# Later places in the instruction order for weight splits, and earlier places for two norm products, in a two-block transformer layer

## Chip, core and metric

The kernel runs on one core of a Trainium2 chip. The metric is the device time of one execution in microseconds (us), lower is better; before is the kernel as it stood, after the kernel with the change. The engines are PE (matmul), PEld (its weight load), DVE (vector), ACT (scalar), POOL (GpSimd) and SP, whose queue here issues the weight loads.

## What is computed

Two blocks one after the other on 512 tokens of width 1024, float32 in and out. Only what the change touches:

```python
# first block, after its mixers
x = x + gate1 * (concat([o_g, o_s]) @ w_out)              # w_out 1024 x 1024
h2 = rms_norm(x, norm2_w) * (1.0 + scale2) + shift2
ffn = (silu(h2 @ w_gate) * (h2 @ w_up)) @ w_down          # 1024 -> 2816 -> 1024
x = x + gate2 * ffn
# second block, with 16 meta tokens ahead of the 512
h = rms_norm_2(concat([meta, x]), pre_norm_g)
z = h @ w_in_2                                            # then split in column groups
(pv, pg, cq, ckv, kr, mg, cu, cg, sbcx, sg, gl) = split_cols(z)
a, gate = split(cu, 2); z = a * sigmoid(gate)             # conformer branch
```

## The kernel before, in words

**Precision by splitting.** Every big float32 product is made of three fp32r matmuls. A weight panel of 128 x 2048 lies in one of three ring buffers; ACT copies it, rounded, to `whi` (`split_hi`, L1422), and DVE subtracts to get `wlo` (`split_lo`, L1932). There are two pairs `whi`/`wlo`, used in turn. `split_hi` and `split_lo` take no name: each call takes the next panel of one fixed list (here `out2`, `out3`, `g0`, `u0`, `g1`, `u1`, `g2`, ...), and it stands in the engine's own order wherever the call stands. Before it writes, ACT waits until PE's last product with the panel two earlier is done (`used`). PE waits for `w_lo` of a panel in `project` (L564) and `first_tiles` (L656). SP loads the panel three later once `w_lo` of a panel is done. Activations are split in the same way (`hi_part` L1426 on ACT, `lo_part` L1937 on DVE).

**Stage A, output projection and second norm.** PE makes eight tiles `mo` 0 to 7 of 128 x 512: 0 to 3 with `out0` and `out1` (L959), 4 and 5 with `out2`, 6 and 7 with `out3` (L569). For each m DVE adds the residual (L2286), ACT squares it (L1660) and writes the rounded, unnormed row `raw_hi` (L1444), POOL adds the squares up (L1349), DVE writes the rest of the row (`raw_rest`, L2005) and goes to m + 1. `out2` is split ahead of m = 0 on ACT and after the residual of m = 0 on DVE.

**A projection ahead of its norm.** The first gate panel `g0` is multiplied with the unnormed rows, chunk by chunk, so that PE has work while the norm is found. Between its chunks PE makes the sums (`norm_stats`, L583 and L586, after chunk 1) and spreads the factor over the partitions (`norm_spread`, L593, after chunk 3). DVE then makes the normed rows (L1996), ACT scales and rounds them (L1433, L1426), DVE makes the rests (L1937), and PE multiplies them with `u0` (L662). The product of `g0` is multiplied by the factor afterwards, in `gate_first_out`, from a copy that ACT takes out of PSUM (`factor_out`, L1441), behind the split of `g1`.

**Stage B, third norm and first panels of the second block.** The same for `cug` (unnormed rows, four tiles `cgate` of 264 columns) and `cu` (normed rows, four tiles). `first_tiles` opens all its PSUM banks before its first matmul. The eight banks go round, and of the four that `cu` opens the last two are those of `cgate` (0,0) and (0,1). Before, ACT copies the four `cgate` tiles out behind its sixth normed row (`both`, L1707), and DVE multiplies the copies by the factor, straight from its PSUM bank, behind all its rests (L2358).

Of the kernel before, what the change touches and what calls it, by code (L numbers as in the profile page):

```python
# [16 lines left out]
D = 1024  # L17
# [98 lines left out]
def program(nc, a, out, known):  # L116
# [3 lines left out]
    with ctx:  # L120
# [13 lines left out]
        def done(stage, *index):  # L134

            return sem(stage), (known[(stage,) + index] if known else 1)
# [128 lines left out]
        hpre3 = arena[:, 0:KD * T].rearrange("p (k t) -> p k t", k=KD)  # L265
        raw3 = arena_r[:, 22 * T:22 * T + 2 * KD * TM].rearrange("p (s k t) -> p s k t", s=2, k=KD)

        factor_of = {"2": arena[:, 36 * T:37 * T]}

        def raw2(s, k):  # L270
            tile = 16 + k if s else k if k < 4 else 8 + k
# [1114 lines left out]
        def _(act):  # L1386
# [28 lines left out]
            def root(tag, out, key, scale, bias):  # L1415
                act.wait_ge(*filled(*key))
                A(out, bank(*key)[0:out.shape[0], 0:out.shape[1]], ACT.Sqrt, bias=bias, scale=scale).then_inc(*read(*key))
# [6 lines left out]
            def hi_part(stage, index, dst, src):  # L1424

                A(dst, src, ACT.Copy).then_inc(*signal(stage + "_hi", *index))  # L1426
# [232 lines left out]
                    act.wait_ge(*done("sqsum" + tag, m - 2))  # L1659
                A(hsq[m % 2] if m else sacc, xT[:, m, :], ACT.Square).then_inc(*signal("xsq" + tag, m))  # L1660

            split_hi()
            for m in range(KD):
                act.wait_ge(*copied("mo", m))
                square_of("2", m)
                act.wait_ge(*done("dve_vectors", "modA2"))
                raw_hi("2", m, modA2[:, m:m + 1])
                if m in (2, 5, 7):
                    split_hi()
            root("2", sroot, ("sum2",), 1.0 / D, epsc)  # L1670
            modulate("2", modA2, 24)
            split_hi()
            factor_out("2")
            for part, (c0, n) in enumerate(FFN_PARTS):
                for i in range(c0 // 2, (c0 + n) // 2):
                    for k in (2 * i, 2 * i + 1):
                        act.wait_ge(*filled("fg", k))
                        if k >= 2:
                            act.wait_ge(*done("a", k - 2))
                        if k < 2:  # L1680
                            act.wait_ge(*copied("fg", k))
                            act.wait_ge(*copied("gshift"))
                            A(silug[k], silug[k], ACT.Silu, bias=gate_bias0[:, k:k + 1]).then_inc(*signal("silug0", k))
                        else:
                            A(silug[k % 2], bank("fg", k)[:, :], ACT.Silu).then_inc(*read("fg", k))
                    if i:
                        split_hi()
                    for k in (2 * i, 2 * i + 1):
                        act.wait_ge(*copied("fu", k))
                        hi_part("a", (k,), act_split[:, 0, k - c0, :], silug[k % 2])  # L1690
                    split_hi()
                for m in range(KD):
                    act.wait_ge(*copied("fd", part, m))
                    if part:
                        if m == 0:
                            for dst in (h_split, raw3):
                                A(dst[:, 0, :, 0:META], hmeta.rearrange("p (k t) -> p k t", k=KD), ACT.Copy)\
                                    .then_inc(*signal("meta_hi"))
                        square_of("3", m)
                        raw_hi("3", m, V1[:, V1_ROWS["pre"] + m:V1_ROWS["pre"] + m + 1])  # L1700
                    split_hi()
            H2 = TM // 2

            def both(key, dst, func=ACT.Copy):
                for half in range(2):
                    act.wait_ge(*filled(*key, half))
                    A(dst[:, half * H2:(half + 1) * H2], bank(*key, half)[:, 0:H2], func).then_inc(*read(*key, half))  # L1707

            root("3", sroot, ("sum3",), 1.0 / D, epsc)
            for k in range(KD):  # L1710
                act.wait_ge(*done("xn3", k))
                hi_part("h3", (k,), h_split[:, 0, k, real], hpre3[:, k, :])
                if k == 5:
                    for m in range(2):
                        both(("cgate", m), conf_gate[m])


            for m in range(2):
                act.wait_ge(*done("cscaled", m))
# [191 lines left out]
        def _(dve):  # L1911
# [76 lines left out]
            def normed_and_rest(tag, first_out, weight=None):  # L1988

                dve.wait_ge(*filled("spread" + tag))  # L1990
                src = bank("spread" + tag)[:, :]
                for k in range(KD + AHEAD):
                    if k < KD:
                        ins = (stt(out=pre_of(tag, k), in0=xT[:, k, :], scalar=col(weight, k), in1=src,
                                   op0=ALU.mult, op1=ALU.mult) if weight else
                               tt(pre_of(tag, k), xT[:, k, :], src, ALU.mult))  # L1996
                        ins.then_inc(*signal("xn" + tag, k))
                    if k >= AHEAD:
                        h_rest(tag, [k - AHEAD])
                first_out()  # L2000

            def raw_rest(tag, k, weight):
                hi = raw_of(tag, 0, k)
# [284 lines left out]

            for m in range(KD):
                residual(("mo", m), m, 16)  # L2290
                if m == 0:
                    split_lo()
                raw_rest("2", m, modA2[:, m:m + 1])
                if m in (3, 5):
                    split_lo()
                if m == 5:
                    dve.wait_ge(*loaded("g0"))
                    for k in range(KD):
                        wk, shift = W("g0")[:, k, :], modT[:, 24 + k:25 + k]
                        if k:  # L2300
                            dve.wait_ge(*done("gate_acc", k - 1))
                            ins = stt(out=gate_acc, in0=wk, scalar=shift, in1=gate_acc, op0=ALU.mult, op1=ALU.add)
                        else:
                            ins = ts(gate_acc, wk, shift, None, ALU.mult)
                        ins.then_inc(*signal("gate_acc", k))

            def gate_first_out():

                split_lo()
                dve.wait_ge(*copied("spread2"))  # L2310
                dve.wait_ge(*filled("gshift"))
                v.tensor_copy(gate_bias0, bank("gshift")[:, 0:2]).then_inc(*read("gshift"))
                for k in range(2):
                    dve.wait_ge(*filled("fg", k))
                    last = tt(silug[k], bank("fg", k)[:, :], factor_of["2"], ALU.mult)
                    last.then_inc(*read("fg", k))

            spread("2", diag)
# [1 line left out]
            normed_and_rest("2", gate_first_out)  # L2320
            for part, (c0, n) in enumerate(FFN_PARTS):
                for i in range(c0 // 2, (c0 + n) // 2):
                    if i:
                        split_lo()
                    if i in (1, 3):
                        ada_sum(10 + i // 2)
                    for k in (2 * i, 2 * i + 1):
                        dve.wait_ge(*(done("silug0", k) if k < 2 else copied("fg", k)))
                        dve.wait_ge(*filled("fu", k))
                        tt(silug[k % 2], bank("fu", k)[:, :], silug[k % 2], ALU.mult).then_inc(*read("fu", k))  # L2330
                    for k in (2 * i, 2 * i + 1):
                        lo_part("a", (k,), act_split[:, 1, k - c0, :], silug[k % 2], act_split[:, 0, k - c0, :])
                    split_lo()
                    if i == 5:
                        ada_mod(10)
                        ada_mod(11)
                        dve.wait_ge(*copied("ada", 11))
                for m in range(KD):
                    residual(("fd", part, m), m, 40)
                    if part:  # L2340
                        if m == 0:
                            dve.wait_ge(*done("meta_hi"))
                            for dst in (h_split, raw3):
                                tt(dst[:, 1, :, 0:META], hm, dst[:, 0, :, 0:META].bitcast(F32), ALU.subtract)\
                                    .then_inc(*signal("h3meta"))
                        raw_rest("3", m, col("pre", m))
                    if not part or m < KD - 1:
                        split_lo()

            H2 = TM // 2  # L2350

            def conf_first_out():

                for m in range(2):
                    for half in range(2):
                        dve.wait_ge(*copied("cgate", m, half))
                    scaled = conf_gate[m][:, META:TM]
                    tt(scaled, scaled, bank("spread3")[:, :], ALU.mult).then_inc(*signal("cscaled", m))  # L2358
                for m in range(2):
                    dve.wait_ge(*done("cscaled", m))  # L2360
                v.engine_nop().then_inc(*read("spread3"))

            spread("3", diag3)
            split_lo()
# [275 lines left out]
```

## Time and profile before

| | us |
|---|---|
| median of 3 executions | 1339.77 |
| lowest, highest | 1338.87, 1343.93 |
| the profiled execution | 1338.87 |
| its span, first to last instruction | 1337.1 |
| PE busy, share of span | 95% |
| mean granted PE clock | 0.985 of full speed |

The page also shows DVE busy for 52% of the span, ACT 37%, PEld 75% and POOL 9%. A busy share is an average over stages. What a moved instruction costs is read from the stretch in which it stands: what PE waits for there, and when. Stage A lies at 362 to 424 us of the span, stage B at 762 to 790 us.

### The profile page before, as it was taken

How to read it: one execution, taken by the hardware profiler on the slowest of the kernel's cores; microseconds unless marked ns; L12 is line 12 of the kernel's file. 1: busy time of each engine (PE TensorE's matmuls, PEld its weight loads, DVE VectorE, ACT ScalarE, POOL GpSimd, SP SyncE). 2: the span in 40 equal slices, each digit the busy share in tenths (PEclk: the TensorE clock that was granted, in tenths of full speed). 3: DMA queues.
4: the chain of work that ended last, by engine and by line, in shares of the span. 5: the costliest groups of instructions: out<-in, count | busy, mean ns of one | idle time of the engine just before them, and what ended most of it. 6: DMA issues, size and time to landing. Idle time of an engine off the chain costs nothing.

```text
span 1337.1 us, 20515 instructions
## 1 busy us (share of the span) xinstructions
PE 1275.0 (95%) x8676; PEld 1008.2 (75%) x8676; DVE 697.3 (52%) x1038; ACT 490.1 (37%) x822; POOL 115.9 (9%) x133
## 2 busy tenths in 40 slices
PE   3899999999989999999999999999899989999996
PEld 2577878889878888888888897986466657677675
DVE  5699878654466443333334588575644333333324
ACT  3544543664345232222223442234445532222232
POOL 4000006411020000000000100000022210000001
PEclk9899999999999999999999999999899999999999
DMA  8665610002022542343322433231301053333211
GB/s 296 217 202 182 220 63 35 3 4 66 1 95 91 162 150 71 95 126 95 95 61 83 140 100 95 86 88 38 71 1 52 1 138 83 83 83 83 83 63 63
DMA packets 141210, 125.77 MB, mean 94 GB/s; under 512 B 6728, under 2 KB 124769, under 8 KB 140992
## 3 DMA queue, kind: packets, MB, share of 16 engines
q1 hardware_dynamic: 137856, 119.62, 29.4%
q0 software_dynamic: 1520, 2.49, 0.6%
q10 hardware_dynamic: 1744, 2.36, 0.5%
q8 instruction: 69, 1.13, 0.4%
q14 instruction: 21, 0.17, 0.0%
HBM read 121.77 MB, written 2.10 MB: 93 GB/s over the span
## 4 chain that ended last, share of the span: by engine, by line
PE 85%; DVE 7%; ACT 3%; DMA 2%; issue 2%; POOL 0%; ACTq 0%; SPq 0%; DVEq 0%; POOLq 0%
PE bank L569 52%; PE bank L810 7%; PE bank L1154 5%; PE bank L662 5%; PE bank L1225 3%; PE bank L1182 2%; PE bank L1136 2%; PE bank L1108 2%; DMA arena<-in_meta_tokens_dram 1%; PE bank L959 1%; DVE wlo L1932 1%; PE bank L1120 1%; PE bank L760 1%; PE bank L782 1%; PE bank L769 1%
## 5 line engine op out<-in xcount | busy, mean ns | idle before, releaser
L569 PE MATMUL bank<-hsplit,whi 128*128 128x512 f32 (+1 forms) x1872 | 561.4, 384 | 0.8 <-DVE wlo L1932 0.7
L569 PEld LDWEIGHTS bank<-hsplit,whi 128*128 128x128 f32 x1872 | 341.6, 188 | 82.3 <-issue 19.0
L569 PE MATMUL bank<-hsplit,wlo 128*128 128x512 f32 (+1 forms) x936 | 352.3, 376 | 0.0
L1932 DVE TENSOR_TENSOR wlo<-ring,whi 128x2048 fp32r<-128x2048 f32 (+4 forms) x90 | 186.6, 2073 | 169.6 <-ACT whi L1422 169.4
L569 PEld LDWEIGHTS bank<-hsplit,wlo 128*128 128x128 f32 x936 | 175.9, 188 | 32.9
L1422 ACT ACTIVATE whi<-ring 128x2048 fp32r<-128x2048 f32 (+4 forms) x90 | 156.3, 1737 | 103.1 <-DVE xT L2286 52.9
L569 PE MATMUL bank<-a_split,whi 128*128 128x512 f32 x340 | 104.7, 389 | 0.0
L2577 DVE TENSOR_TENSOR arena<-bank,tb 128x512 f32<-128x512 f32 x24 | 16.6, 692 | 126.1 <-PE bank L1154 106.2
L1154 PE MATMUL bank<-arena,ring 128*128 128x512 f32 x160 | 75.8, 606 | 1.3 <-DVE arena L2536 1.1
L569 PEld LDWEIGHTS bank<-a_split,whi 128*128 128x128 f32 x340 | 63.8, 188 | 13.2
L1849 ACT ACTIVATE tb<-bank,V 128x512 f32<-128x512 f32 x30 | 20.5, 683 | 138.9 <-PE bank L569 138.9
L569 PE MATMUL bank<-a_split,wlo 128*128 128x512 f32 x170 | 66.1, 389 | 0.0
L1961 DVE SCALAR_TENSOR_TENSOR post<-ring,small,post 128x512 f32<-128x512 f32 x77 | 57.9, 752 | 3.5 <-DMA ring<-in_w_ada_dram 0.8
L1349 POOL TENSOR_TENSOR acc<-acc,tb 128x512 f32<-128x512 f32 x12 | 15.6, 1298 | 434.6 <-ACT tb L1660 434.6
L1154 PEld LDWEIGHTS bank<-arena,ring 128*128 128x128 f32 x160 | 30.1, 193 | 28.6 <-issue 26.5
L1426 ACT ACTIVATE a_split<-tb 128x512 fp32r<-128x512 f32 x22 | 13.8, 632 | 88.4 <-DVE tb L2330 88.3
L2519 DVE TENSOR_TENSOR arena<-arena,consts 128x128 f32<-128x128 f32 x32 | 9.5, 298 | 70.2 <-ACT arena L1818 47.2
L1182 PE MATMUL bank<-hsplit,whi 128*128 128x512 f32 x128 | 44.9, 432 | 0.0
L2286 DVE SCALAR_TENSOR_TENSOR xT<-bank,small,xT 128x512 f32<-128x512 f32 x24 | 17.9, 748 | 50.1 <-PE bank L569 40.1
L1225 PE MATMUL bank<-whi,m_split 128*128 128x512 f32 x128 | 39.6, 390 | 1.7 <-DVE m_split L1937 1.7
L2398 DVE SCALAR_TENSOR_TENSOR arena<-arena,V 128x512 f32<-128x512 f32 x60 | 40.3, 745 | 0.0
L2330 DVE TENSOR_TENSOR tb<-bank,tb 128x512 f32<-128x512 f32 x22 | 14.9, 690 | 48.5 <-PE bank L569 47.0
(430 smaller groups left out, 1786.6 us busy)
## 6 DMA issues: line engine op xcount, KB each, us to landing
ring<-in_w_ada_dram SPq DMA_DIRECT2D x24, 1024.0 KB, 5.3
ring<-in_w_in_dram SPq DMA_DIRECT2D x22, 1024.0 KB, 5.3
ring<-in_w_in_dram SPq DMA_DIRECT2D x34, 512.0 KB, 5.5
ring<-in_w_gate_dram SPq DMA_DIRECT2D x11, 1024.0 KB, 5.3
ring<-in_w_up_dram SPq DMA_DIRECT2D x11, 1024.0 KB, 5.3
ring<-in_w_down_dram SPq DMA_DIRECT2D x8, 768.0 KB, 4.8
ring<-in_w_down_dram SPq DMA_DIRECT2D x8, 640.0 KB, 4.3
ring<-in_w_out_dram SPq DMA_DIRECT2D x4, 1024.0 KB, 5.2
```

Source lines behind the costliest of these rows:

```text
L569: last = mm(o[0:m, 0:n], w[:, k, c0:c0 + m], rhs(s, k), start=k + i == 0, stop=k == kn - 1 and i == 2)
L662: last = mm(o[:, 0:n], w[:, k, c0:c0 + P], rhs(s, k), start=at + i == 0, stop=at == len(order) - 1 and i == 2)
L810: last = mm(o[r, i * width:(i + 1) * width], left[r, n, :], right(n)[r], start=start, stop=stop)
L1108: mm(o[:, 0:m0], q_mla[0:QD, h, i * WIN:(i + 1) * WIN], k_mla[0:QD, h, 0:m0], start=True, stop=True)\
L1136: mm(o[p * HD:(p + 1) * HD, pair * WIN:(pair + 1) * WIN], v_mla[:, c, h * HD:(h + 1) * HD], mpT[u % 2][:, c * WIN:(c + 1) * WIN], start=c ...
L1154: last = mm(o[:, :], W(name)[:, k0 + k, :], ybr[:, kb + k, :], start=k == 0, stop=k == nk - 1)
L1182: last = mm(early[0][:, :], w[:, k, P * (b % 2):P * (b % 2) + P], hx(s, k), start=k + x == 0, stop=k == KD - 1 and x == 2)
L1225: last = mm(fo[b][:, :], mix_split[:, s, 4 * kp + k, b * P:(b + 1) * P], w[:, k, :], start=kp + k + i == 0, stop=kp == 1 and k == 3 and i ...
L1422: split_hi = splitter(act, lambda hi, src: A(hi, src, ACT.Copy), None)
L1932: split_lo = splitter(dve, None, lambda lo, src, hi: tt(lo, src, hi, ALU.subtract))
L1961: last = stt(out=acc, in0=w[:, k, :], scalar=c, in1=acc, op0=ALU.mult, op1=ALU.add)
L2398: stt(out=conf_sum[:, m, :], in0=src, scalar=tap, in1=conf_sum[:, m, :], op0=ALU.mult, op1=ALU.add))
```

## The change

The number of splits and the order of the panels stay. Their places move: `out2` is split after m = 1 on both engines (ACT `m in (1, 3, 5, 7)`, DVE `(1, 3, 5)`), `out3` on ACT after m = 3 rather than m = 2, and `g1` inside the first turn of the FFN loop, on ACT behind the two Silu of that turn and on DVE behind both products with the factor.

The products with the factor (`first_out`) move forward: in `normed_and_rest` they stand ahead of the last two rests, and wait there for ACT's copy of the factor. Stage B gets such a copy too (`factor_of["3"]`). `conf_first_out` now reads `cgate` directly from its four PSUM banks, in halves, multiplies by the copy and so releases the banks on DVE; 16 meta columns are copied unscaled. ACT's four copies of `cgate` are gone.

```diff
-        factor_of = {"2": arena[:, 36 * T:37 * T]}
+        factor_of = {"2": arena[:, 36 * T:37 * T], "3": arena[:, 8 * T:9 * T]}
...
-            split_hi()
             for m in range(KD):
                 act.wait_ge(*copied("mo", m))
                 square_of("2", m)
                 act.wait_ge(*done("dve_vectors", "modA2"))
                 raw_hi("2", m, modA2[:, m:m + 1])
-                if m in (2, 5, 7):
+                if m in (1, 3, 5, 7):
                     split_hi()
             root("2", sroot, ("sum2",), 1.0 / D, epsc)
             modulate("2", modA2, 24)
-            split_hi()
             factor_out("2")
...
-                    if i:
-                        split_hi()
+                    split_hi()
                     for k in (2 * i, 2 * i + 1):
                         act.wait_ge(*copied("fu", k))
...
+            root("3", sroot, ("sum3",), 1.0 / D, epsc)
+            for k in range(KD):
+                act.wait_ge(*done("xn3", k))
+                hi_part("h3", (k,), h_split[:, 0, k, real], hpre3[:, k, :])
+            factor_out("3")
...
-            root("3", sroot, ("sum3",), 1.0 / D, epsc)
-            for k in range(KD):
-                act.wait_ge(*done("xn3", k))
-                hi_part("h3", (k,), h_split[:, 0, k, real], hpre3[:, k, :])
-                if k == 5:
-                    for m in range(2):
-                        both(("cgate", m), conf_gate[m])
...
+                    if k == KD + 1:
+                        dve.wait_ge(*copied("spread" + tag))
+                        first_out(factor_of[tag])
                     if k >= AHEAD:
                         h_rest(tag, [k - AHEAD])
-                first_out()
...
                 residual(("mo", m), m, 16)
-                if m == 0:
-                    split_lo()
                 raw_rest("2", m, modA2[:, m:m + 1])
-                if m in (3, 5):
+                if m in (1, 3, 5):
                     split_lo()
...
-            def gate_first_out():
-
-                split_lo()
-                dve.wait_ge(*copied("spread2"))
+            def gate_first_out(factor):
+
                 dve.wait_ge(*filled("gshift"))
...
-                    if i:
-                        split_lo()
+                    split_lo()
                     if i in (1, 3):
...
-            def conf_first_out():
+            def conf_first_out(factor):
 
                 for m in range(2):
                     for half in range(2):
-                        dve.wait_ge(*copied("cgate", m, half))
-                    scaled = conf_gate[m][:, META:TM]
-                    tt(scaled, scaled, bank("spread3")[:, :], ALU.mult).then_inc(*signal("cscaled", m))
-                for m in range(2):
-                    dve.wait_ge(*done("cscaled", m))
-                v.engine_nop().then_inc(*read("spread3"))
+                        dve.wait_ge(*filled("cgate", m, half))
+                        o, at = bank("cgate", m, half), half * H2
+                        skip = 0 if half else META
+                        if skip:
+                            v.tensor_copy(conf_gate[m][:, 0:META], o[:, 0:META]).then_inc(*signal("part"))
+                        last = tt(conf_gate[m][:, at + skip:at + H2], o[:, skip:H2], factor[:, at + skip - META:at + H2 - META], ALU.mult)
+                        last.then_inc(*read("cgate", m, half))
+                    dve.wait_ge(*copied("cgate", m, 1))
+                    v.engine_nop().then_inc(*signal("cscaled", m))
```

## Rows read from the trace of the kernel before

**Rows 1.** The page's chain that ended last: share of the span by engine

```profile
PE 85%; DVE 7%; ACT 3%; DMA 2%; issue 2%; POOL 0%; ACTq 0%; SPq 0%; DVEq 0%; POOLq 0%
```

**Rows 2.** PE's waits, whole span: who for whom, us in total, times, longest

```profile
PE bank L769 <- POOL wscratch L1306: 3.3, 2, 3.1
...
PE bank L583 <- POOL acc L1349: 2.1, 1, 2.1
...
PE bank L586 <- ACT tb L1660: 1.4, 1, 1.4
```

**Rows 3.** Timeline of DVE, stage A: start, duration, line; idle time before, releaser

```profile
362.44 0.75 DVE L2286 SCALAR_TENSOR_TENSOR xT<-bank,small,xT 128x512 f32<-128x512 f32 x1 [3.30 <-PE bank L959]
365.07 2.29 DVE L1932 TENSOR_TENSOR wlo<-ring,whi 128x2048 fp32r<-128x2048 f32 x1 [1.88 <-ACT whi L1422]
...
367.94 0.75 DVE L2286 SCALAR_TENSOR_TENSOR xT<-bank,small,xT 128x512 f32<-128x512 f32 x1
370.01 1.27 DVE L2005 SCALAR_TENSOR_TENSOR a_split<-xT,small,a_split 128x512 fp32r<-128x512 f32 x1 [1.32 <-ACT a_split L1444]
371.20 0.74 DVE L2286 SCALAR_TENSOR_TENSOR xT<-bank,small,xT 128x512 f32<-128x512 f32 x1
```

**Rows 4.** Timeline of ACT, same stretch

```profile
368.72 0.63 ACT L1660 ACTIVATE tb<-xT 128x512 f32<-128x512 f32 x1 [2.55 <-DVE xT L2286]
369.26 0.71 ACT L1444 ACTIVATE a_split<-xT,small 128x512 fp32r<-128x512 f32 x1
```

**Rows 5.** Timeline of PE: first matmuls of tiles mo 4 and mo 6

```profile
368.36 0.62 PE L569 MATMUL bank<-hsplit,whi 128*128 128x512 f32 x2
...
380.15 0.70 PE L569 MATMUL bank<-hsplit,whi 128*128 128x512 f32 x2 [0.75 <-DVE wlo L1932]
```

**Rows 6.** Windows: PE, PEld, DVE, ACT, POOL busy (instructions); PE clock, DMA share, GB/s

```profile
227.90:234.70 6.80, 6.63 (x78) 4.91 (x78) 4.55 (x15) 2.37 (x8) 4.05 (x6) 0.50 0.01 4
...
398.60:405.40 6.80, 6.80 (x22) 5.74 (x22) 3.92 (x7) 1.95 (x2) 0.00 (x0) 0.50 0.04 5
```

**Rows 7.** Chain that ended last, 398 to 425 us: start, length, matmuls

```profile
400.51 5.19 PE bank L662 x12
...
406.59 2.75 PE bank L662 x12
...
409.68 13.72 PE bank L662 x60
```

**Rows 8.** Timeline of ACT, end of stage A

```profile
417.18 1.90 ACT L1422 ACTIVATE whi<-ring 128x2048 fp32r<-128x2048 f32 x1
418.99 0.57 ACT L1441 ACTIVATE arena<-bank 128x512 f32<-128x512 f32 x1
422.15 1.28 ACT L1683 ACT_TABLE_LOAD   x1 [2.59 <-DVE tb L2315]
423.44 1.34 ACT L1683 ACTIVATE tb<-tb,small 128x512 f32<-128x512 f32 x2
```

**Rows 9.** Timeline of DVE, end of stage A

```profile
406.63 2.48 DVE L1996 TENSOR_TENSOR arena<-xT,bank 128x512 f32<-128x512 f32 x4 [2.49 <-PE bank L593]
...
416.79 1.29 DVE L1937 TENSOR_TENSOR hsplit<-arena,hsplit 128x512 fp32r<-128x512 f32 x2 [0.53 <-ACT hsplit L1426]
...
421.40 1.28 DVE L2315 TENSOR_TENSOR tb<-bank,arena 128x512 f32<-128x512 f32 x2
```

**Rows 10.** Timeline of stage B: PE's first matmul of cu

```profile
777.89 0.48 PE L662 MATMUL bank<-hsplit,whi 128*128 128x264 f32 x2 [1.05 <-ACT arena L1707]
```

**Rows 11.** Timeline of stage B: ACT's last rounded row

```profile
778.83 0.63 ACT L1426 ACTIVATE hsplit<-arena 128x512 fp32r<-128x512 f32 x1 [0.24 <-DVE arena L1994]
```

**Rows 12.** Timeline of DVE, stage B: rests, and four PSUM products of 264 columns

```profile
778.72 2.48 DVE L1937 TENSOR_TENSOR hsplit<-arena,hsplit 128x512 fp32r<-128x512 f32 x4
...
788.79 1.57 DVE L2407 TENSOR_TENSOR arena<-bank,arena 128x264 f32<-128x264 f32 x4 [1.51 <-PE bank L662]
```

**Rows 13.** Chain that ended last, stage B: the matmuls of cu

```profile
777.89 11.88 PE bank L662 x96
```

More of the change, by code:

```diff
@@ L2314, in gate_first_out @@
                     dve.wait_ge(*filled("fg", k))
-                    last = tt(silug[k], bank("fg", k)[:, :], factor_of["2"], ALU.mult)
+                    last = tt(silug[k], bank("fg", k)[:, :], factor, ALU.mult)
                     last.then_inc(*read("fg", k))
```

## The prediction, as it was put on record before the changed kernel ran

> **What bounds the kernel now.** I read the page's chain first: PE makes 85% of it, DVE 7%, ACT 3% [rows 1]. So a moved DVE or ACT instruction costs nothing while PE has work and its full length where PE waits. Next come PE's waits, the few places where it stands. Two are in stage A, 2.1 and 1.4 us ahead of the sums of the second norm; the third shown, 3.1 us on POOL, lies elsewhere and tells what such a gap does to the clock [rows 2]. Then the timelines of stages A and B, engine by engine [rows 3 to 5, 8 to 12]: who is how late. Last the granted clock after gaps [rows 6, 7].
>
> In stage A the reader is to see a chain that goes to and fro between DVE and ACT and not PE: residual 367.94, square 368.72, raw_hi 369.26, raw_rest 370.01, next residual 371.20, so 3.26 us a tile [rows 3, 4]. PE needs 5.4 for a tile (24 matmuls, 0.229 each by 12 in 2.75 [rows 7]), yet the chain also carries splits and ends after PE.
>
> The clock: after the 3.1 us wait and after the two waits of stage A (3.5 us with almost nothing between them) it stood at 0.50 for 6.8 us, that is 1.2 in place of 2.4 GHz; after gaps of 0.75 and 1.05 us no slow stretch followed [rows 2, 5, 6, 10]. At half clock 12 matmuls took 5.19 us, at full clock 2.75 [rows 7]. The slow stretch of stage A cost 2.4 us there and some 0.9 in the sums ahead, 3.3 in all.
>
> **The change part by part.** *1. `out2` split later.* DVE begins at 362.44 with residual 0 [rows 3]. Now no split follows. By the steps of the chain (0.78, 0.54, 0.75) raw_rest 0 starts at 364.5; alone, without POOL beside it, it holds DVE some 0.7 (as the residual, 0.75), so residual 1 is at 365.15, its square at 365.9, raw_hi 1 at 366.5, the ACT split at 367.1. That takes 1.90 [rows 8], so `split_lo` starts at 369.05 and ends 2.29 later [rows 3], at 371.35. PE wants `out2` at 368.36 [rows 5] and starts at about 371.45: a new gap of 3.1 us. Behind the ACT split wait square 2 (not yet possible) and nothing else; behind `split_lo` residual 2, at 371.25 against 371.20 before, so the chain itself loses nothing. SP loads `u0` 4 us later, 20 us ahead of its use.
>
> *2. `out3` on ACT after m = 3.* The chain meets it at 376.45 to 378.35, and `split_lo` starts 0.6 later than before, since it stood ready behind raw_rest 3. PE, late from part 1, reaches tile 6 only at 382.35, so its 0.75 us wait of [rows 5] goes; but chain and sums come 0.6 later.
>
> *3. The gap ahead of the sums.* PE ends its first two chunks 2.2 us later than before and the sums are possible 0.6 later. The gap shrinks from 3.5 to about 2 us. If the clock stays, the 3.3 us of the slow stretch are saved.
>
> *4. What the gap of part 1 does to the clock.* It is as long as the 3.1 us wait of [rows 2], after which the clock fell, so I take a fall here. Then tiles 4 and 5 lose 3.2 us (6.8 us at half clock), of which the chain hands on 1.8: residual 5 waits for its tile until 385.6 rather than 383.8. The square of tile 7 ends 2.4 later than before, at 400.3, the gap ahead of the sums is only some 1 us, and no second fall follows. ACT's split of `u0` moves with the chain and the normed rows (L1996) start at 406.25, not 406.63 [rows 9]. So: no fall at all, L1996 at 404.45 (-2.2); a fall in the new gap, -0.4; a fall only ahead of the sums, +0.6. I take -0.4.
>
> *5. `g1` split behind the Silu.* Relative to L1996 nothing changes until the rests. ACT's copy of the factor moves ahead of the split, to 417.2, and ends at 417.8 (0.57 [rows 8]). DVE, which had two rests to do from 416.79 [rows 9], waits for it, does both products (0.1 + 1.28 [rows 9]), then the rests, until 420.4. PE needs the last two at about 420.7 and 422.1 (6 x 0.229 us a chunk in the 13.72 of [rows 7]): hidden by 0.7 us. ACT loads the Silu table at 418.6, 1.28, then two Silu of 1.34 [rows 8], and only then splits `g1`: 421.2 to 423.1; `split_lo` to 425.4. Before, it was done at 421.4, where the products start [rows 9]; PE finishes `u0` at 423.40 [rows 7] and had 1.8 to spare. Now PE starts at 425.5 when L1996 is where it was. Cost 2.2; with part 4, 1.9 later than before. `u1` comes about 26 us behind `norm_spread` and PE asks for it at 31: hidden by `g1`'s 10.9 us of matmuls.
>
> The Trainium skill, "ScalarE: Activation LUTs" (What ACT_TABLE_LOAD costs), puts a drain of 1.38 us behind each table load, 2.66 in all. Here the Silu starts 1.29 after the load does, so the trace shows no such drain and decides. By the page `g1` would be 1.4 us later still and the sum 1.4 higher.
>
> *6. The clock after the gap ahead of `g1`.* The gap is some 2.5 us. No row shows one of this length: below, 1.05 without a fall, above, 3.1 with one. Bounds 0 and 3.2; I take half, 1.5, because it lies nearer the upper row but not at it.
>
> *7. Stage B.* `cu` cannot start before `cgate` (0,0) and (0,1) are read. Before, ACT did that and PE waited 1.05 us, until 777.89 [rows 10]. Now ACT's last rounded row comes first (778.83, perhaps 0.05 earlier without the copies [rows 11]), then the copy of the factor from 779.4 to 779.95. DVE has done two rests of its four by 779.95 [rows 12] and stands. Then the copy of 16 columns (no row of this shape; below, nothing; above, a quarter of the four products, 0.39; I take 0.1, since it has the fewest columns), 248 and 264 columns, each 0.39 by four in 1.57 [rows 12]: PE starts at about 780.9. Cost 3.0. Nothing behind gives it back: PE is busy without a wait from 777.89 through the 96 matmuls of `cu` [rows 13] and the projections behind, and what waits on ACT and DVE there waits for PE. The Sigmoid and the split of `pv` have 10 us in hand. ACT saves four copies and DVE does 0.4 us more; both hidden by `cu`'s matmuls.
>
> *8. The clock in stage B.* PE now stands 4.1 us, from 776.8 to 780.9, longer than each gap after which the clock fell [rows 2]. Of the 6.8 us slow stretch some lies inside the gap, about 6 behind it. A matmul of `cu` takes 0.124 (96 in 11.88 [rows 13]); at half clock, as estimate by columns from 5.19 / 12 [rows 7], 0.223. 27 of them fit in 6 us and would have taken 3.3: cost 2.7 (bounds 0 and 3.2).
>
> The same skill, "TensorE: Matmul & The Clock Gate" (HAM oscillation), prices a slow stretch at half its length, 3.4 us. My rows give 3.3 and, for the smaller matmuls, 2.7; by the page each of my falls would cost a little more and the sum would be 1.2 higher.
>
> *Sum:* 1.9 + 1.5 + 3.0 + 2.7 = +9.1 us. The profiled execution took 1338.87, 0.9 under the median of the three. 1338.87 + 9.1 = 1348.0.
>
> **The rivals.** *A, the forecast:* both late releases bite and the clock falls in the new gap of tile 4 and in stage B: +7.6 to +11, 1346.5 to 1350. Chance 0.62.
>
> *B, not slower by a measurable amount:* the gaps are there, but the clock pays for them. The slow stretch that stage A has now goes (-3.3) and at most one new one comes. Without any fall: -2.2 + 2.2 + 3.0 = +3.1, 1342; with the one of stage B, +5.7, 1344.6. For it: the gap ahead of the sums does shrink. Against: three gaps of 2.5 to 4 us stand in place of one of 3.5. It decides from +6.7 downward. Chance 0.25.
>
> *C, the moves do nothing or help:* ACT and DVE run ahead further than I count, `out2` and `g1` come in time, and only the lost slow stretch shows: 1336 to 1340. For it: `g1` had 1.8 us to spare. Against: `out2` had 1.0 (367.36 against 368.36), and its split moves by 4. Chance 0.05.
>
> *D, more:* all gaps bring a fall at full price and the sums one too: 1.9 + 3.3 + 3.0 + 3.2, and up to 2 for what slow tiles hand on: +12 to +14, 1351 to 1353. Chance 0.08.
>
> **How the numbers follow.** The likeliest is A, 1348.0. Leaving out what lies under 1342.5 (C and the lowest of B) and over 1352 keeps some 0.85: range 1342.5 to 1352. About 0.5%, 6.7 us, is what a measurement of this kernel can tell from no change. Slower: A, D and none of B, 0.70; same: B and most of C, 0.28; faster: 0.02, since even C gains little.
>
> **What would show it.** In the changed profile: a PE wait of about 3 us on `wlo` at the first matmul of tile 4, none at tile 6; the waits at L583 and L586 together about 1 to 2 us; a wait of 2 to 3 on `wlo` where `g1` begins; a wait of about 4 at the first matmul of `cu`, released by DVE at the `cgate` product and no longer by ACT; windows at clock 0.50 behind the first and the last of these. What would make me wrong: no gap at tile 4 (then part 1's chain is mis-stepped), a fall where I take none or none where I take one, which is worth 3 us each, or stage B's gap given back later.

## The result

| | before | after |
|---|---|---|
| median of 7 executions, us | 1341.07 | 1350.16 |
| lowest to highest | 1338.74 to 1343.93 | 1343.94 to 1353.3 |
| ratio, 95% interval | | 1.0064, 1.0046 to 1.0083 |
| the profiled execution, and its span | 1338.87, 1337.1 | 1351.19, 1349.4 |

The change makes the kernel slower by 0.64%, 9 us; predicted were 1348.0 us, in a range of 1342.5 to 1352.0. The executions of the changed kernel lie 9 us apart, those of before 5. That spread is part of the answer.

The page's chain of the changed kernel, answering to [rows 1]: ACT and DMA have one point more each, PE one less.

```profile
PE 84%; DVE 7%; ACT 4%; DMA 3%; issue 2%; POOL 0%; ACTq 0%; SPq 0%; DVEq 0%; POOLq 0%
```

PE's waits over the whole span, answering to [rows 2]. The waits on `wlo` are new, 5.1 us in two; `cu` waits 4.3 for a DVE product where it waited 1.05 for ACT; the wait at L583 is gone and that at L586 smaller. L769 is as it was.

```profile
PE bank L569 <- DVE wlo L1927: 5.1, 2, 3.0
PE bank L662 <- DVE arena L2353: 4.3, 1, 4.3
...
PE bank L769 <- POOL wscratch L1306: 3.3, 2, 3.1
...
PE bank L586 <- ACT tb L1660: 1.1, 1, 1.1
```

DVE's timeline, answering to [rows 3, 9, 12]. `split_lo` of `out2` at 369.11 rather than 365.07; residual 2 follows at 371.32, against 371.20 before the change; the normed rows start at 409.08, not 406.63; the products with the factor at 420.33 stand ahead of the last two rests; `split_lo` of `g1` comes only at 425.55. In stage B the 16 meta columns and the first two products run from 786.44 on.

```profile
369.11 2.29 DVE L1927 TENSOR_TENSOR wlo<-ring,whi 128x2048 fp32r<-128x2048 f32 x1 [0.53 <-ACT whi L1422]
371.32 0.74 DVE L2283 SCALAR_TENSOR_TENSOR xT<-bank,small,xT 128x512 f32<-128x512 f32 x1
...
409.08 2.48 DVE L1991 TENSOR_TENSOR arena<-xT,bank 128x512 f32<-128x512 f32 x4 [2.86 <-PE bank L593]
...
420.33 1.28 DVE L2308 TENSOR_TENSOR tb<-bank,arena 128x512 f32<-128x512 f32 x2
421.52 1.28 DVE L1932 TENSOR_TENSOR hsplit<-arena,hsplit 128x512 fp32r<-128x512 f32 x2
425.55 2.29 DVE L1927 TENSOR_TENSOR wlo<-ring,whi 128x2048 fp32r<-128x2048 f32 x1 [2.74 <-ACT whi L1422]
...
786.44 0.17 DVE L2352 COPY arena<-bank 128x16 f32<-128x16 f32 x1
786.53 0.75 DVE L2353 TENSOR_TENSOR arena<-bank,arena 128x248 f32<-128x248 f32 x2
```

ACT's timeline, answering to [rows 8, 11]: copy of the factor, table load, two Silu, and only then the split of `g1`; in stage B the last rounded row and the copy of the factor behind it, with which DVE's 786.44 begins.

```profile
419.64 0.58 ACT L1441 ACTIVATE arena<-bank 128x512 f32<-128x512 f32 x1
421.08 1.28 ACT L1681 ACT_TABLE_LOAD   x1 [0.86 <-DVE tb L2308]
422.37 1.34 ACT L1681 ACTIVATE tb<-tb,small 128x512 f32<-128x512 f32 x2
423.61 1.90 ACT L1422 ACTIVATE whi<-ring 128x2048 fp32r<-128x2048 f32 x1
...
785.29 0.63 ACT L1426 ACTIVATE hsplit<-arena 128x512 fp32r<-128x512 f32 x1 [0.63 <-DVE arena L1989]
785.83 0.58 ACT L1441 ACTIVATE arena<-bank 128x512 f32<-128x512 f32 x1
```

PE's timeline at its four waits, answering to [rows 5, 10]: tile 4, the sums, the first matmul with `g1`, the first of `cu`.

```profile
371.55 1.19 PE L569 MATMUL bank<-hsplit,whi 128*128 128x512 f32 x2 [2.96 <-DVE wlo L1927]
...
400.39 0.38 PE L586 MATMUL bank<-consts,tb 128*128 128x1 f32 x2 [1.12 <-ACT tb L1660]
...
427.99 0.70 PE L569 MATMUL bank<-hsplit,whi 128*128 128x512 f32 x2 [2.14 <-DVE wlo L1927]
...
787.64 0.78 PE L662 MATMUL bank<-hsplit,whi 128*128 128x264 f32 x2 [4.33 <-DVE arena L2353]
```

Windows of the changed kernel, columns as in [rows 6]; the number ahead of the last two is the granted clock. Behind each of the four waits there is a stretch at half clock, two of 6.8 us and two of 3.4.

```profile
370.80:377.70 6.90, 6.15 (x15) 4.83 (x16) 4.28 (x5) 3.59 (x5) 2.59 (x2) 0.51 0.48 154
377.70:384.00 6.30, 6.30 (x29) 5.23 (x28) 4.43 (x4) 1.95 (x3) 1.30 (x1) 1.00 0.30 92
401.60:408.40 6.80, 6.80 (x21) 5.64 (x21) 3.39 (x7) 1.30 (x2) 0.00 (x0) 0.50 0.14 21
...
428.90:432.30 3.40, 3.40 (x10) 2.63 (x9) 2.20 (x4) 2.60 (x3) 0.00 (x0) 0.50 0.93 303
787.30:790.70 3.40, 3.06 (x14) 3.09 (x15) 2.93 (x13) 3.38 (x4) 0.00 (x0) 0.50 0.00 0
```

**Where the 12.3 us between the two profiled executions lie.** The same matmul, counted along PE's instructions, at four places:

| | before | after | added since the last |
|---|---|---|---|
| first matmul with `g1` | 423.24 | 427.99 | 4.7 |
| first matmul of `cu` | 777.89 | 787.64 | 5.0: wait 3.3 longer, slow stretch at 428.9 the rest |
| a matmul of the stage behind | 910.11 | 921.19 | 1.3: slow stretch at 787.3 |
| end of the span | 1337.1 | 1349.4 | 1.2 |

The last 1.2 us lie behind both stages; the wait of the attention's transposes for POOL (L1120) is 6.5 there and was 5.2. It does not go with the change: in other profiles it is 6.8 with stage B's changes alone, 6.6 in a version of the kernel before (`gate_acc` behind the spread, below), and 5.0 to 6.0 in the rest that have it.

### The profile page after: what moved, and what is told of

The parts are those of the page before. It is cut to its first block, busy times and chain, and to the rows that moved or that the text cites. A ratio compares the mean times of both kernels' runs of the same rounds, so it can differ in the third digit from the quotient of the medians.

```text
span 1349.4 us, 20515 instructions
## 1 busy us (share of the span) xinstructions
PE 1281.8 (95%) x8676; PEld 1014.3 (75%) x8676; DVE 698.1 (52%) x1042; ACT 489.2 (36%) x819; POOL 116.1 (9%) x133
## 3 DMA queue, kind: packets, MB, share of 16 engines
q10 hardware_dynamic: 1744, 2.36, 0.5%
## 4 chain that ended last, share of the span: by engine, by line
PE 84%; DVE 7%; ACT 4%; DMA 3%; issue 2%; POOL 0%; ACTq 0%; SPq 0%; DVEq 0%; POOLq 0%
PE bank L569 52%; PE bank L810 7%; PE bank L1154 5%; PE bank L662 4%; PE bank L1225 3%; PE bank L1182 2%; PE bank L1136 2%; PE bank L1108 2%; DMA arena<-in_meta_tokens_dram 1%; PE bank L959 1%; DVE wlo L1927 1%; ACT whi L1422 1%; PE bank L1120 1%; PE bank L760 1%; PE bank L620 1%
## 5 line engine op out<-in xcount | busy, mean ns | idle before, releaser
L569 PE MATMUL bank<-hsplit,whi 128*128 128x512 f32 (+1 forms) x1872 | 564.3, 386 | 5.1 <-DVE wlo L1927 5.1
L662 PE MATMUL bank<-hsplit,whi 128*128 128x512 f32 (+1 forms) x128 | 34.3, 360 | 8.3 <-DVE arena L2353 4.3
```

Source lines behind the costliest of these rows:

```text
L569: last = mm(o[0:m, 0:n], w[:, k, c0:c0 + m], rhs(s, k), start=k + i == 0, stop=k == kn - 1 and i == 2)
L662: last = mm(o[:, 0:n], w[:, k, c0:c0 + P], rhs(s, k), start=at + i == 0, stop=at == len(order) - 1 and i == 2)
```

## The experiments

All ratios are against the kernel before, run on the same chip in turn, with 95% intervals. The theory: two weight splits and two PSUM banks are released later than PE wants them, and the clock falls behind the gaps. The rivals: one stage makes all the loss; the gaps alone make it; the moved products and not the split delay PE.

**Each stage alone.** Stage A alone keeps `both` and the product behind the rests in stage B; stage B alone keeps the old places of the splits:

```diff
 # stage A alone, against after
-                    if k == KD + 1:
+                    if k == KD + 1 and tag == "2":
...
-            normed_and_rest("3", conf_first_out, "pre")
+            normed_and_rest("3", None, "pre")
+            conf_first_out()                              # as in before
 # stage B alone, against before
+                    if k == KD + 1 and tag == "3":
+                        dve.wait_ge(*copied("spread3"))
+                        first_out(factor_of["3"])
```

> The changes of stage A alone; stage B as before. My theory (late release of out2 and of g1, plus falls of the clock behind the two gaps): +2 to +6 us over before, middle +3.5; in the trace a wait of 3.0 on wlo at the first matmul of tile 4, 2.1 at the first with g1, and cu at its old wait of 1.0. Rival (stage A's gaps are paid for by the slow stretch that is saved, all of the loss is stage B's): within 1 us of before. Rival (stage A makes it all): +9.

> The changes of stage B alone; stage A as before. My theory: cu's banks come 3.0 to 3.2 us later, and the gap of over 4 us brings one slow stretch worth 1.5 to 2.7: +4.5 to +6 us over before; in the trace a wait of 4.2 at the first matmul of cu, released by DVE. Rival (the gap costs its length alone): +3.1. Rival (given back in the later waits around the attention of the second block): 0 to +1. The parts should add: this and the stage A kernel together within 1.5 us of the whole change's +9.

Stage A alone: 1.0018 (1.0004 to 1.0033), +2.4 us. Stage B alone: 1.0037 (1.0022 to 1.0051), +5.0. Together 7.4, against 8.6 by the ratio of the whole; the intervals overlap. By the medians both stages lose, B more. That stage A makes it all (+9) is out; that it makes less than 1 us is not excluded by its interval alone, which begins at +0.5. The waits are where they were expected: 3.0 at tile 4, 2.4 at `g1` (2.1 expected) and 1.0 at `cu` with stage A alone, 4.34 at `cu` with stage B alone. In the profile of stage A alone the clock fell behind tile 4 and behind `g1`, 3.4 us each, and not behind the sums.

**One release at a time.**

```diff
 # out2 back: ACT splits ahead of m = 0 and at m in (2, 5, 7), DVE at m = 0, 3, 5
+            split_hi()
...
-                if m in (1, 3, 5, 7):
+                if m in (2, 5, 7):
 # g1 early: on ACT behind the copy of the factor, on DVE behind the last rests
             factor_out("2")
+            split_hi()
...
             normed_and_rest("2", gate_first_out)
+            split_lo()
```

> The changed kernel with the splits of out2 and out3 where they stood before; all else as changed. My theory: the gap at tile 4 and its slow stretch go, but the gap of 3.5 us ahead of the sums with its slow stretch comes back, since with full speed tiles PE is early again; so only little is won: 0 to -2 us against the changed kernel, +7 to +9 over before. In the trace: no wait at tile 4, waits of 2.1 and 1.4 at L583 and L586, a slow stretch behind them. Rival (the new gap at tile 4 costs its 3.1 us and its fall's 3.2 in full): -5 to -6 against the changed kernel.

> The changed kernel with the split of g1 directly behind ACT's copy of the factor and ahead of the Silu (DVE: behind the last rests), all else as changed. My theory: wlo of g1 is then ready some 0.5 us ahead of PE's need, the wait of 2.1 goes and with it the fall behind it: -2.2 to -3.8 us against the changed kernel, so +5 to +7 over before. Rival (the products with the factor, moved ahead of the last rests, delay u0 itself): the wait moves to u0's last chunks and nothing is won.

`out2` back: 1.0044 (1.0032 to 1.0056), so 2.7 us less than the whole change by the ratios, between my 0 to 2 and the rival's 5 to 6. The two intervals overlap, so the times alone do not decide between them. The profile does: PE waits as expected, 2.1 and 1.4 ahead of the sums again with a slow stretch of 6.8 behind them, none at tile 4. The 3.0 us at tile 4 are thus mostly a gap moved and not a gap made. `g1` early: 1.0030 (1.0021 to 1.0040), 4.6 us less, and PE's wait on `wlo` at `g1` is gone. That is more than 2.2 to 3.8, within what two intervals allow. The products ahead of the rests stayed where the change puts them, and PE has no wait at the last chunks of `u0`, so they are not what costs; the place of the split behind the Silu is.

**Gaps kept, clock kept.** Matmuls whose results are overwritten stand ahead of the waits, so PE is busy while the splits and banks come as late as in the changed kernel. Shown are those of tile 4 and of `g1`'s first tile:

```diff
+            def filler(o, count):
+                for _ in range(count):
+                    mm(o[:, :], h_even[:, 0, 0, 0:P], h_even[:, 0, 1, :], start=True, stop=True)
...
                 o = open_tile(pe, *key)
+                filler(o, {("mo", 4): 12, ("fg", 2): 9}.get(key, 0))
```

> The changed kernel with matmuls added whose results are overwritten, in the four places where PE waits: 12 of 512 columns ahead of tile 4, 2 and 5 ahead of the sums, 9 ahead of g1's first tile, 30 of 264 columns ahead of cu. They are meant to be a little shorter than each gap, so the gaps stay as late releases and only the clock is kept up. My theory (a part of the loss is the clock): no window at 0.50 in stages A and B, L1991 about 2.2 us earlier than in before, +3 to +4 us over before, so -5 to -6 against the changed kernel. Rival (the clock after such gaps matters little, the loss is the waits): within 1.5 us of the changed kernel, +8 to +10 over before. If fillers run over the gaps they add up to 1 us.

> Stage B's changes alone, with 30 matmuls of 264 columns, overwritten later, ahead of cu, so that PE is busy through most of the 4.3 us wait while cu's banks come as late as before. My theory (the loss of stage B is its wait, 3.2 us, and a slow stretch on top of it): no slow stretch at 780 to 792, +3.2 us over before, some 1.5 less than stage B alone unfilled (+5.0). Rival (the wait alone makes all of stage B's loss): as unfilled, +5.

> The kernel before with 9 and 6 such matmuls of 512 columns in the gap ahead of the sums of the second norm. My theory: the slow stretch behind that gap, 3.3 us, goes: -2.5 to -3.5 us against before. Rival (the clock falls anyway, or the next wait takes the time): 0 to -0.5.

The changed kernel filled: 1.0034 (1.0023 to 1.0045), 4 us less than unfilled (5 to 6 expected). The normed rows start at 405.39, 1.2 us earlier than before where 2.2 were expected. `g1`'s first matmul stands at 424.2, and not at 427.99 as in the first unfilled profile; two later unfilled profiles, below, have it at 423.9 too, so what the fillers are worth is read from the times. Stage B alone, filled: 1.0016 (1.0003 to 1.0028), against 1.0037 unfilled: 2.8 us less, where I expected 1.5 to 1.8; the intervals are wide enough for both, and overlap each other a little. In its profile there is no slow stretch at `cu`, as the first of the next two rows shows, against the unfilled one below it:

```profile
782.00:792.00 10.00, 10.00 (x83) 10.00 (x84) 5.12 (x14) 3.27 (x4) 0.00 (x0) 1.00 0.31 91
```

```profile
783.00:793.00 10.00, 8.72 (x59) 8.75 (x60) 6.15 (x18) 4.32 (x5) 0.00 (x0) 0.83 0.18 47
```

83 matmuls began in ten microseconds with fillers, 59 without; 1.3 us of that second window is the end of the wait. The kernel before, filled, is 0.9977 (0.9967 to 0.9988), 3 us faster than before, with its waits covered and the instructions of the other engines where they were: what was won is the clock. But the fall did not go whole. One slow stretch of 3.4 us, at about 400, in place of 6.8, stayed in both filled kernels of stage A although every wait there was under 0.4 us. The sums themselves stand ahead of it, 16 matmuls of one column in 2.3 us (changed kernel) and 2.1 us (before). The row is of the changed kernel, filled; in the other the clock is 0.57 there too.

```profile
400.00:404.00 4.00, 4.00 (x12) 3.14 (x12) 3.13 (x6) 0.81 (x2) 0.00 (x0) 0.57 0.01 4
```

**The same kernel again.** Two more profiles of the changed kernel, unedited.

> The changed kernel once more, unedited, for one look. My theory (the late releases are fixed, the falls of the clock behind them are not the same in every execution): waits at tile 4, g1 and cu as in the first profile within 0.1 us (3.0, 2.1, 4.3), but slow stretches of another number or length, and the span different by their cost, 1 to 5 us. Rival (the falls are fixed too and the executions differ for another reason): the same stretches as in the first profile.

> The same once more: the waits within 0.1 us of the first profile's, the slow stretches different from it or from the other look in number or length.

The waits at tile 4 (2.96) and at `cu` (4.33) are the same in all three profiles. That at `g1` is 2.14, 2.36 and 2.14, in the second profile 0.2 longer where 0.1 was allowed, and those ahead of the sums are 1.1, 1.1 and 2.0 together:

```profile
PE bank L569 <- DVE wlo L1927: 5.3, 2, 3.0
```

```profile
PE bank L569 <- DVE wlo L1927: 5.1, 2, 3.0
PE bank L586 <- ACT tb L1660: 1.4, 1, 1.4
PE bank L583 <- POOL acc L1349: 0.6, 1, 0.6
```

The slow stretches are not:

| slow stretch, us | tile 4 | sums | `g1` | `cu` | `g1` at | span |
|---|---|---|---|---|---|---|
| first profile | 6.8 | 6.8 | 3.4 | 3.4 | 427.99 | 1349.4 |
| second profile | 3.4 | none | none | 3.4 | 423.92 | 1342.8 |
| third profile | none | 3.4 | 3.4 | 6.8 | 423.87 | 1345.9 |

One program, spans up to 6.6 us apart, and they stand in the order of the time at half clock in the two stages: 20.4 us of it with 1349.4, 13.6 with 1345.9, 6.8 with 1342.8. The twenty recorded executions of this program, which have a mean granted clock each, say the same: the three at 0.984 took 1343.9 to 1347.0 us, the eight at 0.980 or below 1350.1 to 1354.0. The late releases come with the order of the instructions and differ by 0.2 us; only the sums' wait depends on whether the clock fell before it. The falls vary.

Absolute times of two executions differ by what happened earlier in them, by some 3 us at most. Counted from PE's last matmul of tile 3 (at 368.13 before) to the first with `g1`, stage A took

| | us | slow stretches on the way, us |
|---|---|---|
| before; stage B alone, with the stage A of before | 55.1; 55.1 | 6.8; 6.8 |
| changed: first, second, third profile | 59.8, 55.6, 56.5 | 13.6, 3.4, 3.4 |
| stage A alone | 55.6 | 3.4 |
| `out2` back | 57.4 | 6.8 |

So up to `g1`, with its late split, stage A lost 4.7 us in the first profile, but 0.5 to 1.4 in the other three: there the slow stretch of 6.8 us that before has at the sums is partly saved. And with `out2` back the way is longer than in those three. In these profiles the later split of `out2` costs this stretch something only where the clock fell both at tile 4 and at the sums.

**A version that beats both.** The old gap ahead of the sums comes from eight `gate_acc` instructions of 3.9 us behind m = 5, in the to and fro of DVE and ACT. First they went behind the spread, then, two at a time, into DVE's waits for ACT:

```diff
                 residual(("mo", m), m, 16)
                 if m == 0:
                     split_lo()
+                if m == 4:
+                    dve.wait_ge(*loaded("g0"))
+                for k in range(2 * m - 8, 2 * m - 6) if m >= 4 else ():
+                    ...                                   # step k of gate_acc
                 raw_rest("2", m, modA2[:, m:m + 1])
```

> The kernel before with the eight DVE instructions of the gate's shift (gate_acc, 3.9 us) moved from behind m = 5 to behind the spread of the second norm's factor. By the to and fro of DVE and ACT, the square of tile 7 is then done 3.9 us earlier, when PE has just finished its first two chunks: the gap ahead of the sums and its slow stretch go, some of it given back because the normed rows now wait for gate_acc and the split of u0: -4 to -6 us against before. Rival (u0's split, now behind gate_acc, is late and opens a gap of its own): -1 to -3.

> The kernel before with the eight gate_acc instructions put two at a time into DVE's waits for ACT (1.3 us each) behind the residuals of m = 4 to 7. My theory (DVE's order ahead of the sums and ahead of the normed rows sets both gaps): sums as early as in the kernel with gate_acc behind the spread (395.5 us), no gate_acc between the spread and the normed rows, so L1996 at about 399 and no wait at u0's first chunk: -3 to -4 us against that kernel, -7 to -9 against before, no window at 0.50 from 390 to 425. Rival (the two steps stretch the to and fro by what they take, so each tile comes 0.2 to 1 later): -5, as that kernel.

Behind the spread: 0.9960 (0.9947 to 0.9973), 1335.39 us, with a wait of 1.9 at `u0`'s first chunk and a slow stretch of 3.4 behind it, the gap that the rival named; the gain is in the range forecast all the same. In the waits: 0.9946 (0.9930 to 0.9961), 1333.29 us, 7 us faster than before, as forecast, and 1.2% faster than after. Against the kernel with `gate_acc` behind the spread it is 2 us less, where I expected 3 to 4; the intervals are wide enough for both. Its chain through the sums has no wait and no slow stretch; 12 matmuls take 2.86 and 2.73 us on either side of the spread, against 5.19 and 2.75 in [rows 7].

```profile
398.23 2.86 PE bank L662 x12
401.09 0.89 PE bank L593 x8
401.98 2.73 PE bank L662 x12
```

## Why the prediction was right

*Part 1, `out2`.* `split_lo` forecast for 369.05, measured 369.11; PE's start 371.45 against 371.55. The first `raw_rest` took 0.75 with POOL idle, where those beside a POOL addition take 1.27, as assumed. *Part 2.* No wait at tile 6, as said. *Part 3.* In the third profile, where the clock did not fall at tile 4, the gap ahead of the sums is 0.6 + 1.4 = 2.0, as forecast.

*Part 4, the clock at tile 4.* The fall came in two of three profiles of the changed kernel, 6.8 us long in the first and 3.4 in the second, and in the first one residual 5 waited for its tile, until 385.60, with 385.6 forecast. But "no second fall follows" failed: with only 1.1 us of wait ahead of the sums the clock fell for 6.8 us, and the normed rows started at 409.08, not at 406.25. That is the step that went wrong: I had priced a second fall at nothing because the wait ahead of the sums would be short. With that same wait of 1.1 the clock fell behind the sums in the first profile and with `g1` early, and not in the second profile nor with stage A alone, so it is a matter of the execution. That term is -0.4 in the sum and was +2.45 in the first profile. In the second, with a fall of 3.4 at tile 4 alone, the rows started at 405.03, so it was -1.6 (-1.8 when counted from tile 3; the forecast had -2.2 for a run without any fall). In the third, with 3.4 at the sums alone, it was -0.9 counted so, where a whole stretch of 6.8 had been put at +0.6.

*Part 5, `g1`.* Forecast 2.2; PE waited 2.14 and started 2.3 later than before relative to the normed rows, and the chain from the normed rows to `g1`'s first matmul took 18.9 us with 18.9 forecast. The Silu started 1.29 us after its table load again, so the drain that the Trainium skill gives there ("ScalarE: Activation LUTs", What ACT_TABLE_LOAD costs) did not show. *Part 6.* Taken at half of 3.2; measured 3.4 us long in two profiles and absent in one, some 1.7 us when it came; with stage A alone and with `out2` back it came too, 3.4 each. The 1.5 was right by luck: I had meant half a chance of a full stretch of 6.8, and what came was half a stretch in four profiles of five.

*Part 7, stage B.* Forecast 3.0, measured 4.33 - 1.05 = 3.3. The steps on ACT and DVE took what was forecast, 0.09 for the 16 columns among them; the rest is between the end of DVE's second product (787.28) and PE's first matmul (787.64), 0.36 where I had allowed 0.1. *Part 8.* The clock fell in all six profiles with stage B's changes and no fillers, but the stretch was 3.4 long in four of six; it cost 1.3 to 1.5 then (from the first matmul of `cu` to the mark at 910.11, against before), and 2.5 to 2.6 where it was 6.8. The term of 2.7 was mis-sized, about twice too big for four of the six: the price of a whole stretch was right, its length was not.

So the waits were right to 0.3 us, and that is the forecast's merit. That the sum of 9.1 matches the measured 9.1 (by medians) and 8.6 (by the ratio) so closely is luck in part: two errors in the clock cancel, a fall in stage A that may or may not come and a stretch in stage B that is too long. From tile 3 to the mark at 910.11 the three profiles of the changed kernel add 11.0, 5.2 and 8.9 us to before. So the forecast fits the middle of executions that differ by more than its terms. Of the rivals, B is what some executions show: the second profile, span +5.7, and the lowest of the seven at 1343.94. D is what others show: the first profile, with a fall at all four places, the sums included, took 1351.19, and three of the seven lie above 1351. C is out, for no profile lacks the waits.

The rule of the Trainium skill that a slow stretch costs half its length ("TensorE: Matmul & The Clock Gate", HAM oscillation) would give, as an estimate, 1.7 for 3.4 us and 3.4 for 6.8; behind `cu`, 1.3 to 1.5 and 2.5 were measured. In four of the six profiles 0.4 to 1.2 us of the stretch lie in the wait itself, and a matmul of 264 columns takes 0.22 in it, less than twice its 0.124.

## What to carry to other kernels

When a split or a copy is moved behind another engine's chain, write down when the consumer wants it and step the chain to it; its slack before (1.0 us for `out2`, 1.8 for `g1`) tells more than its cost. A bank handed back by a later reader is a delay too, even when ACT saves four copies by it. Price the clock apart from the gap, as a thing that comes in some executions, and read a loss by it from more than one profile. A short wait is no reason to rule a fall out where a run of one-column matmuls stands beside it, as the sums here show. Here work with no consumer near was best put in an engine's waits, not between two steps of a chain.

## What the runs showed of the chip

The same program had slow stretches of none, 3.4 or 6.8 us at the same place in different executions, at tile 4 behind the same wait of 2.96 us. Behind the old gap of 3.5 us at the sums the clock fell in all four profiles that have it (6.8, 6.8, 6.8 and, with stage B filled, 10.2 us). A fall followed the sums with every wait around them under 0.4 us, but none followed in the version with `gate_acc` in the waits, nor in two profiles with a wait of 1.1. Why the one and not the other stays open. The DVE copy of 128 x 16 from PSUM is 0.17 long and the next instruction starts 0.09 after it.
